# Two transformer blocks on one core: mixes, gates and head outputs in PSUM, the root of one norm applied behind its matmuls, a moved wait, and squares added by one engine

## What is computed

```python
# block one; 16 meta tokens stand ahead of the 256
n = rms(h, norm_mix_w)
q, k, v, glu, g_att, g_conv = split(n @ w_in)
y_att  = rms(diff_attention(q, k, v), subln_w) * (1 - lambda_init)
u      = silu(layernorm(causal_dwconv31(glu_a * sigmoid(glu_b))))
y_conv = u @ w_conv_out
m      = sigmoid(g_att) * y_att + sigmoid(g_conv) * y_conv      # the mix
h      = h + m @ w_out
up     = causal_dwconv3(rms(h, norm_ffn_w) @ w_up)              # 3 taps along the tokens
gate, val = split(up)                                           # 2816 channels each
h      = h + (silu(gate) * val) @ w_down
# block two
xn  = rmsnorm(h, norm_mix_g)
y_a = moba_attention(q_a, k_a, v_a) @ w_br_attn                 # 16 heads
fg  = lb + (1 - lb) * sigmoid(f_b);  kh = 1 - fg;  logf = log(fg)
o   = hgrn2_scan(q_b, kh, i_b, logf)                            # 8 heads of 128
o   = o * rsqrt(mean(o*o per head) + eps) * norm_g * silu(og_b)
y_b = o @ w_br_hgrn
h   = h + (sigmoid(g_a) * y_a + sigmoid(g_b) * y_b) @ w_out
h   = h + memory_cross_attention(rmsnorm(h), rmsnorm(mem))
h   = h + (silu(gate) * up) @ w_ffn_out                         # of rmsnorm(h) @ w_ffn_in
out = rmsnorm(h, final_norm_g)
```

## Time and profile before

| | us |
|---|---|
| median of 3 runs | 1185.38 (1184.91 to 1185.74) |
| the profiled execution | 1185.46 |
| its span in the trace | 1183.8 |
| TensorE busy | 1142.3 (96%) |
| VectorE (DVE) busy | 738.6 (62%) |
| GpSimd (POOL) busy | 654.3 (55%) |
| ScalarE (ACT) busy | 601.5 (51%) |

### The profile page before, as it was taken

One profiled execution on the slowest core, in us unless ns is written; L12 is line 12 of the kernel. 1 busy time (PEld: TensorE's weight loads), 2 busy tenths in 40 slices (PEclk: granted clock), 3 DMA queues, 4 the chain that ended last, 5 costly groups with the idle time before them and its releaser, 6 DMA issues.

```text
span 1183.8 us, 24898 instructions
## 1 busy us (share of the span) xinstructions
PE 1142.3 (96%) x8962; PEld 1095.9 (93%) x8962; DVE 738.6 (62%) x1362; ACT 601.5 (51%) x1120; POOL 654.3 (55%) x455
## 2 busy tenths in 40 slices
PE   6999999999989999999899999999989999999997
PEld 6999999998889999999899999898979989999996
DVE  5675756688857777427775757576697546444322
ACT  5644444445346565337645454555535455444332
POOL 4666666660356666545654636373665436656642
PEclk9999999999989999999999999999989999999998
DMA  8443444442344545543433334233435435555541
GB/s 324 146 143 142 157 141 162 142 148 72 143 178 145 192 168 194 189 148 138 143 143 127 126 116 162 101 113 142 179 107 179 143 107 179 182 179 206 179 143 36
DMA packets 26209, 179.43 MB, mean 152 GB/s; under 512 B 2848, under 2 KB 4128, under 8 KB 4768
## 3 DMA queue, kind: packets, MB, share of 16 engines
q1 hardware_dynamic: 25856, 178.28, 42.0%
q10 hardware_dynamic: 288, 0.27, 0.1%
HBM read 177.49 MB, written 1.05 MB: 151 GB/s over the span
## 4 chain that ended last, share of the span: by engine, by line
PE 74%; DVE 11%; issue 7%; POOL 4%; ACT 2%; DVEq 0%; DMA 0%; POOLq 0%; ACTq 0%
PE ps L567 51%; PE ps L845 10%; POOL parts L417 2%; PE ps L923 2%; PE ps L662 1%; DVE act L1806 1%; DVE work L2166 1%; PE ps L633 1%; PE ps L607 1%; ACT parts L1116 1%; DVE branch L1947 1%; PE ps L916 1%; POOL res L2379 1%; DVE work L1713 1%; PE ps L690 1%
## 5 line engine op out<-in xcount | busy, mean ns | idle before, releaser
L417 POOL TENSOR_TENSOR parts<-ring,parts 128x1024 fp32r<-128x1024 f32 x208 | 513.8, 2481 | 470.7 <-ACT parts L1116 467.7
L567 PE MATMUL ps<-x_high,parts 128*128 128x256 f32 (+2 forms) x3088 | 417.6, 284 | 3.4 <-DVE glu L1982 2.0
L567 PEld LDWEIGHTS ps<-x_high,parts 128*128 128x128 f32 x3088 | 387.1, 189 | 14.4 <-issue 8.1
L1116 ACT ACTIVATE parts<-ring 128x1024 fp32r<-128x1024 f32 x324 | 323.9, 1049 | 136.9 <-PE ps L845 69.3
L417 DVE TENSOR_TENSOR parts<-ring,parts 128x1024 fp32r<-128x1024 f32 x116 | 151.8, 1308 | 127.3 <-ACT parts L1116 127.3
L567 PE MATMUL ps<-x_low,parts 128*128 128x256 f32 (+2 forms) x1520 | 214.5, 284 | 0.0
L567 PEld LDWEIGHTS ps<-x_low,parts 128*128 128x128 f32 x1520 | 196.3, 189 | 0.0
L1733 DVE SCALAR_TENSOR_TENSOR ps<-glu,table_sb,ps 128x256 f32<-128x256 f32 x232 | 93.3, 480 | 0.6 <-DVE ps L1733 0.2
L845 PE MATMUL ps<-act_high,parts 128*128 128x256 f32 x704 | 87.8, 279 | 0.0
L845 PEld LDWEIGHTS ps<-act_high,parts 128*128 128x128 f32 x704 | 85.1, 188 | 0.0
L567 PE MATMUL ps<-parts,x_high 128*128 128x256 f32 x448 | 62.3, 285 | 0.9 <-DVE work L2081 0.9
(11 more groups left out here) (330 smaller groups left out, 1660.3 us busy)
## 6 DMA issues: line engine op xcount, KB each, us to landing
ring<-weights SPq DMA_DIRECT2D x166, 1024.0 KB, 4.8
res<-h_in SPq DMA_DIRECT2D x4, 272.0 KB, 3.6
act<-mem SPq DMA_DIRECT2D x1, 1024.0 KB, 14.8
out<-xT SPq DMA_DIRECT2D x4, 256.0 KB, 2.5
table_sb<-table SPq DMA_DIRECT2D x1, 969.5 KB, 9.1
table_sb<-table ACTq DMA_DIRECT2D x1, 132.5 KB, 3.4
work<-positions ACTq DMA_DIRECT2D x1, 128.0 KB, 4.4
```

The source lines that it names most:

```text
L417: eng.tensor_tensor(parts[:, LOW - HIGH + p, cols], ring[:, slot, cols], parts[:, p, cols].bitcast(F32), ALU.subtract)\
L567: mm = pe.matmul(out, left(k), right(k), start=step_ == 0 and k == 0, stop=step_ == 2 and k == KB - 1)
L1116: sc.activation(parts[:, p, cols], ring[:, slot, cols], ACT.Copy).then_inc(split_high, 1)
```

## The change

**Squares.** For mix1 and the last norm the DVE adds all eight squares, and TensorE sums one tile. At the end POOL's additions go; the DVE adds squares between its additions of down2's tiles. The norm of `ffn1` leaves the list of those that are made token-wise (NORMS).

**Mix of block one.** Gate and sum are formed in place in the PSUM bank of conv_out's tile; ACT's `mixed_high` and the DVE's low part read it there. The bank is free only when the low part is made, so TensorE waits for `x_low_ready` ahead of tiles 4 to 7.

**First feed-forward norm.** It takes the raw form. The raw high part lies in `ffn_high`, in the place of `conv`. Each of the 44 tiles of up1 is multiplied in PSUM by the inverse root, by a new instruction of the DVE, and ACT's first tap waits for it. The order in a group of four becomes scale 0, taps 0, scale 1, taps 1, scale 2, low half, taps 2, scale 3, product 2, taps 3, product 3, low half.

**forget.** `kh` is made first, the forget gate stays in PSUM, and the clip writes `bT` from there; ACT's logs wait for the banks. TensorE's waits for banks 2 and 3 move from ahead of the loop heads2 into `rotate` and the second group of `hgrn_scores`.

**Head outputs.** All eight head sums follow one another, two heads per bank in banks 4 to 7; the roots (ACT), the reciprocals (DVE, two heads each) and both products stay in PSUM, and POOL's four products go to the DVE. ACT rounds two heads at a time, the DVE subtracts two at a time. Their order among the gates of branch_a is new. The first chunk of branch_b is made by `split_late` with two k blocks late.

**Mix of block two.** As that of block one, in PSUM, with the same kind of wait for tiles 4 to 7 and ahead of mix_out2.

The core of the diff:

```diff
+            def mixed_read(which, t):
+                if t >= 4:
+                    pe.wait_ge(x_low_ready, INPUTS[which] * KB + t - 3)
             def tile(phase, i, t, moving, width, ready=None):
                 hold(pe, tile_read[b], STREAM.before(phase, i, t))
+                mixed_read("mixed1", t)
...
+                if which == "mixed1":
+                    pe.wait_ge(x_low_ready, INPUTS[which] * KB + 6)
                 products(high, high_x, range(KB - late), begin=True)
...
-            token_sum_of_two(TQ, "ffn1")
-            inverse_spread(4, TQ)
             def ffn(up, down, width, count):
-                if up == "up1":
-                    split_chunk(up, 0, 0, width, first=INPUTS["ffn1"] * KB)
-                else:
-                    split_raw(up, "ffn2", x_high, x_low, width)
+                raw_high = ffn_high if up == "up1" else x_high
+                split_raw(up, "ffn" + up[-1], raw_high, x_low, width)
...
             def rotate(i, src, t):
+                hold(pe, tile_read[2], STREAM.before("branch_a", 0, 2))
...
-            for b in (2, 3):
-                hold(pe, tile_read[b], STREAM.before("branch_a", 0, b))
...
-            head_sums(lambda j: sq[:, j, 0:SEQ], SEQ, squared)
+            for h in range(HEADS):
+                b = 4 + h // 2
+                pe.wait_ge(squared, n.next(squared))
+                pe.matmul(ps[:, b, h % 2 * SEQ:(h % 2 + 1) * SEQ], ones, sq[:, h, 0:SEQ], start=True, stop=True)\
+                  .then_inc(head_summed, 1)
...
-            split_chunk("branch_b", 0, 0, SEQ, first=INPUTS["oh"] * KB, x_high=oh_high, x_low=oh_low)
+            last_products = split_late("branch_b", oh_high, oh_low, SEQ, "oh", 2)
...
-                        sc.wait_ge(tile_done, STREAM.done(phase, i, t))
+                        sc.wait_ge(scaled, n.next(scaled))
                         act_fn(taps[:, 4 * (g % 2) + e, :], ps[:, bk, 0:SEQ], ACT.Identity, tap0,
...
-                ve.scalar_tensor_tensor(xT[:, t, 0:TQ], gates[:, KB + t, :], 1.0, ps[:, b, 0:TQ], ALU.add, ALU.mult)\
+                ve.scalar_tensor_tensor(z, gates[:, KB + t, :], 1.0, z, ALU.add, ALU.mult).then_inc(tile_read[b], 1)
                 ve.wait_ge(tile_read[b], STREAM.before("conv_out", 0, t) + 1)
-                ve.tensor_tensor(xT[:, t, 0:TQ], xT[:, t, 0:TQ], att[:, t, :], ALU.add).then_inc(mixed, 1)
+                ve.tensor_tensor(z, z, att[:, t, :], ALU.add).then_inc(mixed, 1)
...
+                def scale(e):
+                    t, b, _ = tile_at(e)
+                    ve.wait_ge(tile_done, STREAM.done(phase, i, t))
+                    ve.tensor_tensor(ps[:, b, 0:TQ], ps[:, b, 0:TQ], rinv[:, 0:TQ], ALU.mult).then_inc(scaled, 1)
...
+                scale(0)
+                convolve(0)
+                scale(1)
+                convolve(1)
+                scale(2)
+                behind(phase, i, tile_at(1)[0] // 2, "up1")
+                convolve(2)
+                scale(3)
+                gated(2)
+                convolve(3)
+                gated(3)
+                behind(phase, i, tile_at(3)[0] // 2, "up1")
...
+                step(ve.tensor_scalar(kh[:, t, :], z, minus_key[:, t:t + 1], key[:, t:t + 1], ALU.mult, ALU.add))
+                step(ve.tensor_scalar(z, z, one_lb[:, t:t + 1], lb[:, t:t + 1], ALU.mult, ALU.add))
+                ve.tensor_scalar(bT[:, t, :], z, LOG_MIN, None, ALU.max).then_inc(tile_read[b], 1)
...
+            def gate_b(pair):
+                ve.wait_ge(head_rooted, pair + 1)
+                step(ve.reciprocal(ps[:, 4 + pair, :], ps[:, 4 + pair, :]))
+                for h in (2 * pair, 2 * pair + 1):
+                    ins = ve.scalar_tensor_tensor(head_at(h), oh[:, h, :], hgrn_g[:, h:h + 1], head_at(h), ALU.mult, ALU.mult)
...
+                    ve.tensor_tensor(head_at(h), head_at(h), og[:, h, :], ALU.mult).then_inc(hgrn_ready, 1)
...
             gate_a(range(2))
+            gate_b(0)
+            gate_b(1)
+            gate_a(range(2, 4))
+            gate_b(2)
+            low_b(0)
+            low_b(1)
+            gate_a(range(4, 6))
+            gate_b(3)
+            low_b(2)
+            gate_a((6,))
+            low_b(3)
+            gate_a((7,))
```

199 lines of the change are left out of this document (93 added, 106 removed).

## The result

The changed kernel takes **1194.83 us** (median of 5 runs, 1194.18 to 1196.88) against 1185.38 for the kernel before, run beside it: the ratio is 1.0079, with a 95% interval from 1.0068 to 1.0090. It is slower by 9.4 us. 1187.2 was forecast with a range from 1179 to 1211; the result lies in that range and above 1193, the upper end of the forecast's own narrower range (without its rivals).

The account below looks back on a forecast made before the run. TensorE, busy for 96% of the span, was taken as the bound, so only changes that move it count. The terms -0.7 + 5.5 - 6.5 + 8.7 + 0.3 - 5.0 - 0.6 gave +1.7: 1187.2 us, range 1179 to 1211.

Parts of the forecast that it names:

- rival A: In up1, the DVE's low half loses its 0.08 lead and waits for POOL, +23 us: 1210 us, chance 0.27.
- First norm: At the first norm, one more DVE square but 6 TensorE records instead of 12: -0.7 us.
- tail: At the kernel's end, fewer TensorE records but later DVE sums: -0.6 us (-0.9 to -0.2).
- Mix of block one: From conv_out through mix_out1, TensorE waits for banks and later DVE work: +5.5 us (3.0 to 6.4).
- The step on conv_out: Before conv_out's tile 5, TensorE waits for a low part issued behind gate_heads(1): +3.6 us.
- the step on mix_out1: Before mix_out1's third chunk, work comes 3.4 us later, raw copies add 0.8; TensorE stands about 3, clock another 1.3.
- Norm ahead of up1: Between mix_out1 and up1's first chunk, the raw norm takes 6.9 us instead of 13.4: -6.5 us.
- Scaling in up1: In up1, scaling makes a DVE-ACT chain of 12.5 us per group: +8.7 us (+5 to +11).
- forget: From forget into heads2, TensorE's wait moves, the clip avoids POOL, the clock may fall: +0.3 us (-0.8 to +1.4).
- Branches: In block two's heads and branches, PSUM forms and paired reciprocals shorten the DVE's chain: -5.0 us (-6.5 to -3.0).
- B: In up1, TensorE's pace is kept and the scaling costs about 0: 1178.5 us, chance 0.22.
- C: In the branches, PSUM forms are still blocked by POOL, gain about 0: 1192 us; chance 0.08 with other slower sums.

Follow-up runs that it names:

- the kernel with the gains alone: The changed kernel with block one's mix, up1's norm and groups, and the moved waits ahead of heads2 undone together: 1178.59 us, 0.9948 of the kernel before.

## Why the prediction was right or wrong

The result lies in the stated range because that range was stretched to 1211 for rival A, which did not happen; it is outside the forecast's own 1181 to 1193. Of the 7 us between forecast and trace, 6.7 are one term, up1. Two further misses, +1.5 behind forget and -1.5 in the branches, cancel by luck: both are for the most part the granted clock, which fell where 0.8 was allowed for it and did not fall where 1.3 was.

- **What bounds the kernel** was right: every engine's busy time fell and the time rose; each term was a wait of TensorE at a handover or, in up1, its supply.
- **First norm, tail**: -0.60 and -0.53, forecast -0.7 and -0.6.
- **Mix of block one**: +5.40, forecast +5.5. The step on conv_out is confirmed to 0.1 us (3.51 for 3.6), and undoing its cause took it away. So are the parts of the step on mix_out1: the later queue of the DVE gave 3.8 (forecast 3.4), the raw copies 0.79 (forecast 0.8), and what follows, clock and waits together, 0.84 (forecast 1.3).
- **Norm ahead of up1**: -6.84, forecast -6.5. 0.9 of it is a longer low stretch of the clock in the kernel before; against the run with the norm undone it is 5.94.
- **Scaling in up1**: +15.4, forecast +8.7 (its own 132.0 less 123.2 is 8.8), beyond its upper bound of 11. The mechanism was right (the chain with ACT, because scale and convolution stand back to back), and the size was off by a single link: the scale's start to the tap's, 0.46 in the sum, is 0.67 in the loop. It stands three times in a group, and three times 0.21 on 12.53 is 13.16, against 13.18 measured. The 0.46 had been taken as an operation's length and 0.03, which holds where addresses are constants. With ACT's loop written out the link is 0.46 and up1 133.25, 1.3 over the 132.0 of the sum. The bound of 0.3 per group was too narrow for a chain of some fifteen links, each read from one row.
- **forget**: to the third tile of heads2 +0.30. The clock behind the single wait cost 1.51 and not 0.8, so the term is +1.8, over its bound of 1.4. The further +0.56 in the stretch from down1 to forget is a low stretch of the clock that came earlier in the norm there; no edit touches it, other runs have between -0.04 and +1.56 there, and its cause stays open.
- **Branches**: -6.49, forecast -5.0 with -6.5 as the end. gate_b and the end of the wait were right to 0.3; the 1.3 for the clock was not charged in the profiled run.
- **PSUM forms cost like SBUF forms**: confirmed. The subtraction L1833, from PSUM, takes 0.42 with 258 columns, as L1818 did from SBUF, and the scale, PSUM to PSUM, 0.42 to 0.43. By the Trainium skill (VectorE: DVE Perf Modes, the section on the TRN2 errata: 120 fixed cycles for a PSUM source, 58 for SBUF) the PSUM form should take some 0.065 more, an estimate from the page; these rows do not show it.
- **Rivals.** A did not happen: the lead was 0.12 and not the 0.08 of the sum, and even 0.08 would have held, as 0.07 did in every trace; 0.27 was too high a chance. The edge, put at about 0.05, is at 0.04. Its mechanism is real and its price was near (2.5 for 2.3 per group), and the kernel was one small instruction from it. B did not happen as it stood, but it is what the order with the scales ahead gives: 1180.5 us, forecast for B 1178.5. C did not happen: the products from PSUM run beside POOL unhindered (two at 867.01 in 0.76, within POOL's low part of 866.79 to 869.19).

## What to carry to other kernels

A new operation put between a producer and its consumer on two engines costs its links, not its length: 44 operations of 0.43 us cost 15 us where each waited for the other engine and 1.5 us where the next one was issued ahead. Before costing such a chain, read each link from a row that has the same kind of addressing, since register instructions behind the wait add to it in a loop only. And look at who stands behind a long instruction whenever a wait is put on a result that used to be free to come late.

A wait is no measure of the work behind it, since it is only what is left when TensorE arrives. Waits of 0.15, 1.65 and 2.44 stood ahead of mix_out1's third chunk, which came at the same time behind tables1 in the first two kernels and 0.79 later in the third. Compare when the work behind the wait starts.

## What was not expected of the hardware

- The same wait of 2.75 or 2.76 us in the same place (branch_b's first chunk) was followed by a low granted clock in three of the thirteen traces, with 1.5 us lost, and by none in the others. Waits of this size are a risk of 1.5 us, not a price.
- A slow stretch of the clock is nearly free if a wait for something else follows soon: 0.4 us behind forget, and nothing in mix_out1 of the kernel before. That takes 25.62 with a low stretch and a wait of 0.15; the kernel with the gains alone takes the same 25.62 with no low stretch and a wait of 1.65.
- Which of two low parts is held turned on 0.3 us: with the DVE 0.12 ahead POOL loses 0.86 per group, off the path; with POOL 0.21 ahead the DVE loses 2.2, on the path. The edge is at a recorded lead of the DVE of 0.040.
